# Stick-breaking attention: the values' products of two key blocks issued one behind the other

## The chip, the cores and the metric

The kernel runs on one core of a Trainium2 chip. Its time is the device time of one execution in microseconds (us); a kernel is timed several times and the median is given.

## What is computed

Three transformer blocks are applied to a sequence of 512 tokens of width 1024, all in float32. The first has stick-breaking attention with 16 heads of 64, the second has differential attention, the third mixes pooling, attention and a state-space scan; each ends in a gated feed-forward. The change touches only the attention of the first block:

```python
def block(args):
    q_blk, blk = args
    q_pos = blk * Q_BLOCK + jnp.arange(Q_BLOCK, dtype=jnp.int32)
    z = jnp.einsum('bqhd,bkhd->bhqk', q_blk, k, preferred_element_type=jnp.float32) * scale
    earlier = key_pos[None, :] < q_pos[:, None]
    log_keep = jnp.where(earlier, jax.nn.log_sigmoid(-z), 0.0)
    log_after = lax.cumsum(log_keep, axis=3, reverse=True) - log_keep
    weight = jnp.where(earlier, jnp.exp(jax.nn.log_sigmoid(z) + log_after), 0.0)
    return jnp.einsum('bhqk,bkhd->bqhd', weight.astype(v.dtype), v)
```

Every score z needs its softplus, and every weight needs the sum of the softplus values of all later keys. So the keys have to be gone through from the last to the first.

## The kernel before

TensorE (PE), VectorE (DVE), ScalarE (ACT) and the DMA queue (SP) each have a program of their own, written out by hand; semaphores tie them together. No scheduler moves anything: PE executes in the order in which the source names its steps.

Matrices with float32 accuracy are multiplied in three parts, since each operand is kept as a high and a low half: part 0 is high by high, part 1 the input's low half by the weights' high half, part 2 the input's high half by the weights' low half. `product` (line 1826) issues such a product of eight rows of 128 for one tile of 128 output columns: per part eight matmuls of 128x512 (L1844). `linear(n, j, parts)` is that product for head pair n, with j = 0, 1, 2 for query, key and value. The result is taken out of PSUM by DVE (`qkv_tile`, L1087), which also scales it.

The first block's attention runs over eight pairs of heads, n = 0 to 7. `pair(n, last)` in `stick_breaking` goes through the four key blocks of 128 of one pair, g = 0 to 3, from the last keys to the first. Key block g is seen by 128, 256, 384 or 512 queries. For each g:

- `scores(n, g)`: two matmuls of 64 contraction rows, one for each head of the pair, run side by side on the two halves of the array's rows (L1909), and then two small ones that add the mask (L1912). They write the PSUM pair `S2[g % 2]`.
- ACT's `soften(n, g)` (L589, L591, L593) takes the absolute value, the exponential and the logarithm of it. DVE's `softplus(n, g)` (L1101, L1103, L1105) finishes the softplus and splits it into `soft_hi` and `soft_lo`. For g = 0 to 2, DVE's `fold(n, g)` (L1113, L1116, L1119, L1121) adds up what the next key block needs, in the tile `later`.
- `exponents(n, g)`: PE adds the sums over later keys into the same PSUM pair: four matmuls from `soft_hi` and `soft_lo` (L1922), and for g > 0 two from `later` (L1927), with a wait of its own ahead of them.
- ACT's `weights(n, g)` (L598) takes the exponential and writes `wgt`. It signals `sb_w`.
- `weigh(n, g)`: two matmuls with 64 output columns, one for each head, run side by side on the two halves of the array's columns (L1940). They add up the output of the pair in the PSUM bank `ob`. They wait for `sb_w` (L1937), and for g = 0 also for `sb_o` (L1935, the bank `ob` has been read) and `sb_vt` (L1936, the values have been turned). Behind g = 3, DVE's `output(n)` reads `ob` (L1126, L1128).

`scores(n, g)` reuses a PSUM pair and so waits (L1906) until `weights` of two key blocks before has read it. `scores(n, 2)` therefore has the same condition on `sb_w` as `weigh(n, 0)`, `scores(n, 3)` as `weigh(n, 1)`, `scores(n + 1, 0)` as `weigh(n, 2)`, and `scores(n + 1, 1)` as `weigh(n, 3)`.

Between these steps of pair n, PE's program has parts of the query, key and value products of pair n + 1 (`fill`); in the last pair, parts of the output projection (`begin_out`, L1870) stand there. DVE's order in one pair is: softplus 1, fold 0, a weight split (L968), softplus 2, fold 1, the query tile, a split, the key tile (L1087), softplus 3, fold 2, a split, softplus 0 of pair n + 1, the value tile, `output(n)`, `values(n + 1)`. Each DVE instruction waits for the one before it where it reads its result.

Of the kernel before, what the change touches and what calls it, by code (L numbers as in the profile page):

```python
# [154 lines left out]
def three_blocks(nc, tables, x, positions, attn_norm, w_in, w_out, q_norm, k_norm, lambda_q1, lambda_k1,  # L155
# [19 lines left out]
    with ctx:  # L175
# [1647 lines left out]
        def _(pe):  # L1823
# [34 lines left out]
            def begin_out(l, f, parts, rows=range(KT - 1)):  # L1858

                u, acc = At(U_WO[l] + f), out_bank(l, f)  # L1860
                wh, wl = w_hi[u.slot], w_lo[u.slot]
                for part in parts:
                    if part == 0:
                        pe.wait_ge(hi_ready, u.of(1, 1))
                        if f < 2 and 0 in rows:
                            pe.wait_ge(evac, V_WO[l] + f + 1)
                    if part == 2:
                        pe.wait_ge(lo_ready, u.of(1, 1 + CREDIT))
                    for k in rows:
                        ins = pe.matmul(acc[:, :], (wh, wh, wl)[part][:, k, :], (o_hi, o_lo, o_hi)[part][:, k, :],  # L1870
                                        start=part == 0 and k == 0, stop=False, skip_group_check=True)
                if f < 2 and 2 in parts and KT - 2 in rows:
                    ins.then_inc(lin_done, 1)
# [27 lines left out]
            def stick_breaking(u0, v0, late):  # L1901
                def scores(n, g):

                    j = NB - 1 - g
                    pe.wait_ge(evac, n.of(3, v0 + 2 + CREDIT))
                    pe.wait_ge(sb_w, (n.scale(4) + g).of(1, 1))  # L1906
                    for a in range(2):
                        k = slice(64 * a, 64 * a + 64)
                        pe.matmul(S2[g % 2][:, a, 0:SPAN[j]], kb[n.slot][k, P * j:P * j + P], qb[n.slot][k, P * j:SEQ],  # L1909
                                  start=True, stop=True)  # L1910
                    for a in range(2):
                        ins = pe.matmul(S2[g % 2][:, a, 0:P], mask("ident"), mask("hide_sb"), start=False, stop=True,  # L1912
                                        skip_group_check=True)
                    ins.then_inc(sb_z, 1)

                def exponents(n, g):

                    j = NB - 1 - g
                    pe.wait_ge(sb_soft, n.of(SB_SOFT[NB], SB_SOFT[g + 1]))
                    for a in range(2):  # L1920
                        for part in (soft_hi, soft_lo):
                            ins = pe.matmul(S2[g % 2][:, a, 0:SPAN[j]], table_r("neg_from"), part[:, a, OFF[j]:OFF[j] + SPAN[j]],  # L1922
                                            start=False, stop=True, skip_group_check=True)
                    if g:
                        pe.wait_ge(sb_later, n.of(SB_LATER[NB - 1], SB_LATER[g]))
                        for a in range(2):
                            ins = pe.matmul(S2[g % 2][:, a, P:SPAN[j]], table_r("neg_all"),  # L1927
                                            later[:, a, LATER[g - 1]:LATER[g - 1] + SPAN[j + 1]],
                                            start=False, stop=True, skip_group_check=True)
                    ins.then_inc(sb_exp_in, 1)  # L1930

                def weigh(n, g):
                    j = NB - 1 - g
                    if g == 0:
                        pe.wait_ge(sb_o, n.of(2, 1))  # L1935
                        pe.wait_ge(sb_vt, n.of(1, 1))  # L1936
                    pe.wait_ge(sb_w, (n.scale(4) + g).of(1, 1 + CREDIT))  # L1937
                    for a in range(2):
                        cols = slice(64 * a, 64 * a + 64)
                        ins = pe.matmul(ob[cols, P * j:SEQ], vt[n.slot][:, j, cols], wgt[:, a, OFF[j]:OFF[j] + SPAN[j]],  # L1940
                                        start=g == 0, stop=g == NB - 1, skip_group_check=True)
                    if g == NB - 1:
                        ins.then_inc(sb_pv, 1)

                def turn_values(n):
                    pe.wait_ge(evac, n.of(3, v0 + 3 + CREDIT))
                    pe.wait_ge(sb_vt, n.of(1))
                    for b in range(NB):
                        ins = pe.transpose(misc[:, b * P:(b + 1) * P], vf[:, b * P:(b + 1) * P], table("ident"))
                    ins.then_inc(sb_vtr, 1)  # L1950

                def linear(n, j, parts=(0, 1, 2), late=None):
                    product(n.scale(3) + (u0 + j), n.scale(3) + (v0 + j), h_hi, h_lo, parts=parts, late=late)

                def pair(n, last):

                    def fill(j, parts):
                        if not last:
                            linear(n + 1, j, parts)
                        else:  # L1960
                            if j == 0 and 0 in parts:
                                pe.wait_ge(sb_o, n.of(2, 1))
                            if j == 2 and 0 in parts:
                                pe.wait_ge(sb_vt, n.of(1, 1))
                            begin_out(0, j, parts)
                    exponents(n, 0)
                    fill(0, (0,))
                    weigh(n, 0)
                    scores(n, 2)
                    fill(0, (1, 2))  # L1970
                    exponents(n, 1)
                    fill(1, (0,))
                    weigh(n, 1)
                    scores(n, 3)
                    fill(1, (1, 2))
                    exponents(n, 2)
                    fill(2, (0,))
                    weigh(n, 2)
                    if not last:
                        scores(n + 1, 0)  # L1980
                    fill(2, (1,))
                    exponents(n, 3)
                    fill(2, (2,))
                    weigh(n, 3)
                    if last:
                        begin_out(0, 3, (0,))
                    if not last:
                        scores(n + 1, 1)
                        turn_values(n + 1)
# [27 lines left out]
                turn_values(At(0))  # L2017
                pe.wait_ge(vec_ready, 2)
                by_two(pe, KT, pair)

            def differential(u0, v0, late):
# [457 lines left out]
```

## Time and profile before

| what | value |
|---|---|
| median of 3 runs | 2180.82 us (2180.41 to 2181.83) |
| the profiled execution's own time | 2181.55 us |
| its span on the core | 2179.8 us |
| granted TensorE clock, mean | 0.998 of full speed |
| PE busy | 2155.2 us (99%) |
| DVE busy | 1418.8 us (65%) |
| ACT busy | 792.1 us (36%) |
| DMA | 188.31 MB, mean 86 GB/s |

The span is what the profiler saw on the core from the first to the last instruction. Busy shares are of the span. Matmuls overlap in the records, since the next is issued before the one before has left the array; so the cost of a matmul in a row of matmuls is read from start to start. Where a timeline row says "x4" for two matmuls in the program, it is because a float32 matmul shows as two passes.

### The profile page before, as it was taken

How to read it: one execution, taken by the hardware profiler on the slowest of the kernel's cores; microseconds unless marked ns; L12 is line 12 of the kernel's file. 1: busy time of each engine (PE TensorE's matmuls, PEld its weight loads, DVE VectorE, ACT ScalarE, POOL GpSimd, SP SyncE). 2: the span in 40 equal slices, each digit the busy share in tenths (PEclk: the TensorE clock that was granted, in tenths of full speed). 3: DMA queues.
4: the chain of work that ended last, by engine and by line, in shares of the span. 5: the costliest groups of instructions: out<-in, count | busy, mean ns of one | idle time of the engine just before them, and what ended most of it. 6: DMA issues, size and time to landing. Idle time of an engine off the chain costs nothing.

```text
span 2179.8 us, 28415 instructions
## 1 busy us (share of the span) xinstructions
PE 2155.2 (99%) x10090; PEld 1720.2 (79%) x10090; DVE 1418.8 (65%) x2154; ACT 792.1 (36%) x1165; POOL 0.2 (0%) x4
## 2 busy tenths in 40 slices
PE   8999999999999999999999999999999999999998
PEld 6666788888887777888888877777788888888887
DVE  7888855554448897655554486687755567888733
ACT  6555422222225555322222234366622223222222
POOL 0000000000000000000000000000000000000000
PEclk9999999999999999999999999999999999999999
DMA  4212233333332222333333322222233333333332
GB/s 145 58 58 58 68 97 96 96 96 92 97 93 58 67 68 59 104 97 97 96 95 88 102 77 59 58 78 69 68 97 96 97 100 93 96 96 96 102 97 92
DMA packets 367252, 188.31 MB, mean 86 GB/s; under 512 B 8984, under 2 KB 366409, under 8 KB 367177
## 3 DMA queue, kind: packets, MB, share of 16 engines
q1 hardware_dynamic: 367177, 187.30, 30.1%
q8 instruction: 49, 0.80, 0.2%
q14 instruction: 26, 0.21, 0.0%
HBM read 185.18 MB, written 2.10 MB: 86 GB/s over the span
## 4 chain that ended last, share of the span: by engine, by line
PE 89%; DVE 7%; ACT 2%; issue 1%; DMA 0%; SPq 0%; DVEq 0%; ACTq 0%
PE lin L1844 79%; PE S L2029 1%; PE S L1909 1%; DVE conv L1486 1%; PE ob L2064 1%; PE lin L1870 1%; PE ob L1940 1%; ACT w_hi L553 1%; PE S L1870 1%; ACT L838 0%; PE misc L2042 0%; PE S L2205 0%; DVE soft_lo L1105 0%; DVE soft L1101 0%; PE ob L2230 0%
## 5 line engine op out<-in xcount | busy, mean ns | idle before, releaser
L553 ACT ACTIVATE w_hi<-raw 128x1024 fp32r<-128x1024 f32 x361 | 381.5, 1057 | 831.8 <-PE lin L1844 806.5
L968 DVE TENSOR_TENSOR w_lo<-raw,w_hi 128x1024 fp32r<-128x1024 f32 x361 | 441.1, 1222 | 208.2 <-ACT w_hi L553 206.7
L1844 PE MATMUL lin<-h_hi,w_hi 128*128 128x512 f32 x1928 | 490.8, 396 | 0.4
L1844 PE MATMUL lin<-h_lo,w_hi 128*128 128x512 f32 x1928 | 485.0, 393 | 0.0
L1844 PE MATMUL lin<-h_hi,w_lo 128*128 128x512 f32 x1928 | 477.9, 390 | 0.0
L1844 PEld LDWEIGHTS lin<-h_hi,w_hi 128*128 128x128 f32 x1928 | 359.3, 189 | 81.6 <-issue 8.0
L1844 PEld LDWEIGHTS lin<-h_hi,w_lo 128*128 128x128 f32 x1928 | 361.0, 188 | 74.4
L1844 PEld LDWEIGHTS lin<-h_lo,w_hi 128*128 128x128 f32 x1928 | 358.9, 188 | 76.7 <-issue 3.8
L1844 PE MATMUL lin<-gu_lo,w_hi 128*128 128x512 f32 x528 | 131.4, 389 | 0.0
L1844 PE MATMUL lin<-gu_hi,w_lo 128*128 128x512 f32 x528 | 131.4, 389 | 0.0
L1844 PE MATMUL lin<-gu_hi,w_hi 128*128 128x512 f32 x528 | 131.3, 389 | 0.0
L1310 DVE TENSOR_TENSOR up<-lin,rsB 128x512 f32<-128x512 f32 x44 | 30.4, 692 | 134.5 <-PE lin L1844 134.5
L1844 PEld LDWEIGHTS lin<-gu_hi,w_lo 128*128 128x128 f32 x528 | 99.1, 188 | 20.6
L1844 PEld LDWEIGHTS lin<-gu_lo,w_hi 128*128 128x128 f32 x528 | 99.1, 188 | 20.5
L1844 PEld LDWEIGHTS lin<-gu_hi,w_hi 128*128 128x128 f32 x528 | 99.1, 188 | 20.5
L1693 DVE SCALAR_TENSOR_TENSOR cout<-cpad,vec,cout 128x512 f32<-128x512 f32 x88 | 66.2, 752 | 12.0 <-DVE cout L1690 1.5
L1307 DVE TENSOR_TENSOR gate<-lin,rsB 128x512 f32<-128x512 f32 x44 | 30.4, 692 | 62.9 <-PE lin L1844 57.9
L558 ACT ACTIVATE sq<-xt 128x512 f32<-128x512 f32 x32 | 20.3, 633 | 130.8 <-DVE xt L986 94.5
L1657 DVE TENSOR_TENSOR g_raw<-lin,rsB 128x512 f32<-128x512 f32 x21 | 14.5, 692 | 51.3 <-PE lin L1844 51.3
L589 ACT ACTIVATE soft_t<-S 128x256 f32<-128x256 f32 (+3 forms) x32 | 22.6, 707 | 56.7 <-PE S L1912 56.6
L986 DVE TENSOR_TENSOR xt<-lin,xT 128x512 f32<-128x512 f32 x24 | 16.6, 692 | 39.9 <-PE lin L1844 39.9
L889 ACT ACTIVATE gate_s<-cout 128x512 f32<-128x512 f32 x22 | 14.0, 634 | 71.2 <-DVE cout L1693 71.2
(400 smaller groups left out, 2203.1 us busy)
## 6 DMA issues: line engine op xcount, KB each, us to landing
raw<-in_w_in_dram SPq DMA_DIRECT2D x108, 512.0 KB, 3.7
raw<-in_w_gate_dram SPq DMA_DIRECT2D x44, 512.0 KB, 3.8
raw<-in_w_up_dram SPq DMA_DIRECT2D x44, 512.0 KB, 3.8
raw<-in_ffn_up_dram SPq DMA_DIRECT2D x44, 512.0 KB, 3.8
raw<-in_w_down_dram SPq DMA_DIRECT2D x32, 512.0 KB, 3.8
raw<-in_w_out_dram SPq DMA_DIRECT2D x24, 512.0 KB, 3.7
raw<-in_ffn_down_dram SPq DMA_DIRECT2D x16, 512.0 KB, 3.7
raw<-in_w_down_dram SPq DMA_DIRECT2D x16, 384.0 KB, 3.4
```

Of the source, the lines that this page charges most:

```text
L553: act.activation(w_hi[u.slot][:, :, :], raw[u.slot][:, :, :], ACT.Copy).then_inc(hi_ready, 1)
L589: act.activation(soft_j, S2[g % 2][:, :, 0:SPAN[j]], ACT.Abs).then_inc(sb_soft_t, 1)
L968: dve.tensor_tensor(w_lo[u.slot][:, :, :], raw[u.slot][:, :, :], w_hi[u.slot][:, :, :].bitcast(f32), ALU.subtract).then_inc(lo_ready, 1)
L1307: dve.tensor_tensor(gate[:, :], lin[v.slot][:, :], rsB[:, :], ALU.mult).then_inc(evac, 1)
L1310: dve.tensor_tensor(up[:, :], lin[(v + 1).slot][:, :], rsB[:, :], ALU.mult).then_inc(evac, 1)
L1486: s.did(dve.scalar_tensor_tensor(conv[:, :], convB[:, k:k + SEQ], w[k], conv[:, :], ALU.mult, ALU.add))
L1693: s.did(dve.scalar_tensor_tensor(cout[j][:, :], cpad[j][:, k:k + SEQ], col[k], cout[j][:, :], ALU.mult, ALU.add))
L1844: ins = pe.matmul(acc, (wh, wh, wl)[part][:, k, :], (hi, lo, hi)[part][:, k0 + k, :], start=first and part == 0 and k == 0, stop=last and ...
L1870: ins = pe.matmul(acc[:, :], (wh, wh, wl)[part][:, k, :], (o_hi, o_lo, o_hi)[part][:, k, :], start=part == 0 and k == 0, stop=False, skip_ ...
L1909: pe.matmul(S2[g % 2][:, a, 0:SPAN[j]], kb[n.slot][k, P * j:P * j + P], qb[n.slot][k, P * j:SEQ], start=True, stop=True)
L1940: ins = pe.matmul(ob[cols, P * j:SEQ], vt[n.slot][:, j, cols], wgt[:, a, OFF[j]:OFF[j] + SPAN[j]], start=g == 0, stop=g == NB - 1, skip_gr ...
L2029: pe.matmul(dst[:, 0:N], qb[n.slot][rows_, P * i:P * i + P], kb[n.slot][rows_, 0:N], start=True, stop=True)
```

## The change

Only the order in which `pair` issues its steps on PE is changed. `weigh(n, 0)` is moved behind `exponents(n, 1)` and the first part of the next product, directly ahead of `weigh(n, 1)`. `weigh(n, 2)` is moved to the end of the pair, directly ahead of `weigh(n, 3)`. The numbers of instructions on every engine are the same, and the orders on DVE, ACT, GpSimd and the DMA queue are the same.

```diff
                     exponents(n, 0)
                     fill(0, (0,))
-                    weigh(n, 0)
                     scores(n, 2)
                     fill(0, (1, 2))
                     exponents(n, 1)
                     fill(1, (0,))
+                    weigh(n, 0)
                     weigh(n, 1)
                     scores(n, 3)
                     fill(1, (1, 2))
                     exponents(n, 2)
                     fill(2, (0,))
-                    weigh(n, 2)
                     if not last:
                         scores(n + 1, 0)
                     fill(2, (1,))
                     exponents(n, 3)
                     fill(2, (2,))
+                    weigh(n, 2)
                     weigh(n, 3)
```

PE in the first half of a pair in the loop, before. `ob<-wgt,vt` is `weigh`, `S<-qb,kb` with `S<-masks` is `scores`, `lin<-h_hi,w_hi` is part 0 of a product and `lin<-h_lo,w_hi` part 1; the rows without a matmul are the register instructions of a wait.

```order
L1844 MATMUL lin<-h_hi,w_hi_54 128x512 x8
L1935 REGISTER_ALU
L1936 REGISTER_ALU
L1937 REGISTER_ALU
L1940 MATMUL ob<-wgt,vt_94 64x128 x2
L1909 MATMUL S<-qb_89,kb_91 128x384 x2
L1912 MATMUL S<-masks 128x128 x2
L1844 MATMUL lin<-h_lo,w_hi_54 128x512 x8
```

And in the changed kernel, the same place and then the place to which the step went:

```order
L1844 MATMUL lin<-h_hi,w_hi_54 128x512 x8
L1906 REGISTER_ALU
L1909 MATMUL S<-qb_89,kb_91 128x384 x2
L1912 MATMUL S<-masks 128x128 x2
L1844 MATMUL lin<-h_lo,w_hi_54 128x512 x8
```

```order
L1844 MATMUL lin<-h_hi,w_hi_54 128x512 x8
L1935 ISA
L1936 ISA
L1940 MATMUL ob<-wgt,vt_93 64x128 x2
L1937 REGISTER_ALU
L1940 MATMUL ob<-wgt,vt_93 64x256 x2
L1909 MATMUL S<-qb_88,kb_90 128x512 x2
```

The 128-query product has left its place ahead of the scores of key block 2 and stands directly ahead of the 256-query product.

PE in the second half of a pair, from the product of 384 queries to the matmuls on `later`, before:

```order
L1940 MATMUL ob<-wgt,vt_93 64x384 x2
L1909 MATMUL S<-qb_89,kb_91 128x128 x2
L1912 MATMUL S<-masks 128x128 x2
L1844 MATMUL lin<-h_lo,w_hi_55 128x512 x8
L1919 REGISTER_ALU
L1922 MATMUL S<-soft_hi,exact 128x512
L1922 MATMUL S<-soft_lo,exact 128x512
L1922 MATMUL S<-soft_hi,exact 128x512
L1922 MATMUL S<-soft_lo,exact 128x512
L1925 REGISTER_ALU
L1927 MATMUL S<-later,exact 128x384 x2
```

And in the changed kernel, from the matmuls on `later` on:

```order
L1927 MATMUL S<-later,exact 128x384 x2
L1840 REGISTER_ALU
L1844 MATMUL lin<-h_hi,w_lo_57 128x512 x8
L1940 MATMUL ob<-wgt,vt_93 64x384 x2
L1937 REGISTER_ALU
L1940 MATMUL ob<-wgt,vt_93 64x512 x2
L1909 MATMUL S<-qb_89,kb_91 128x256 x2
```

The 384-query product stood ahead of the wait for `later` (L1925) and now stands behind it, after one more part of a product.

## Rows read from the trace of the kernel before

**Rows 1.** The page: the span, and the busy time of each engine.
```profile
span 2179.8 us, 28415 instructions
PE 2155.2 (99%) x10090; PEld 1720.2 (79%) x10090; DVE 1418.8 (65%) x2154; ACT 792.1 (36%) x1165; POOL 0.2 (0%) x4
```

**Rows 2.** Waits from 30 to 256 us: waiting and releasing line: total us, times, longest.
```profile
DVE kb L1087 <- PE lin L1844: 15.8, 7, 2.5
PEld S L1927 <- DVE later L1121: 4.8, 8, 0.9
```

**Rows 3.** PE, one pair: start us, duration us, engine, line, operation, tiles, shapes, count.
```profile
119.95 0.44 PE L1940 MATMUL ob<-wgt,vt 128*64 128x128 f32 x4
120.32 0.92 PE L1909 MATMUL S<-qb,kb 64*128 64x384 f32 x4
...
127.63 0.65 PE L1940 MATMUL ob<-wgt,vt 128*64 128x256 f32 x4
128.21 1.13 PE L1909 MATMUL S<-qb,kb 64*128 64x512 f32 x4
...
133.12 0.34 PE L1922 MATMUL S<-soft_hi,exact 128*128 128x384 f32 x1
...
136.00 0.87 PE L1940 MATMUL ob<-wgt,vt 128*64 128x384 f32 x4
136.79 0.49 PE L1909 MATMUL S<-qb,kb 64*128 64x128 f32 x4
...
139.70 0.40 PE L1922 MATMUL S<-soft_hi,exact 128*128 128x512 f32 x1
139.94 0.39 PE L1922 MATMUL S<-soft_lo,exact 128*128 128x512 f32 x1
140.46 0.62 PE L1927 MATMUL S<-later,exact 128*128 128x384 f32 x2
...
142.86 1.08 PE L1940 MATMUL ob<-wgt,vt 128*64 128x512 f32 x4
143.87 0.70 PE L1909 MATMUL S<-qb,kb 64*128 64x256 f32 x4
```

**Rows 4.** DVE in the same pair; in brackets its idle time and the releaser.
```profile
133.31 0.69 DVE L1087 SCALAR_TENSOR_TENSOR kb<-lin,rsB 128x512 f32<-128x512 f32 x1 [2.47 <-PE lin L1844]
133.92 1.22 DVE L1101 SCALAR_TENSOR_TENSOR soft<-S,soft_t 128x1024 f32<-128x1024 f32 x1
...
135.90 1.23 DVE L1105 TENSOR_TENSOR soft_lo<-soft,soft_hi 128x1024 fp32r<-128x1024 f32 x1
...
139.45 0.95 DVE L1121 TENSOR_TENSOR later<-soft_t,later 64x768 fp32r<-64x768 f32 x1
```

**Rows 5.** ACT in the same pair: the weights of key blocks 0 and 2.
```profile
119.16 0.36 ACT L598 ACTIVATE wgt<-S 128x256 f32<-128x256 f32 x1
...
134.25 0.81 ACT L598 ACTIVATE wgt<-S 128x768 f32<-128x768 f32 x1 [1.44 <-PE S L1927]
```

**Rows 6.** PE in the third block: products of 512, 384, 256, 128 columns back to back.
```profile
1326.23 2.37 PE L2230 MATMUL ob<-fprobT,fvt 128*64 128x512 f32 x16
1328.54 0.42 PE L2242 MATMUL misc<-tab,fd_z 16*128 16x16 f32 x4
```

**Rows 7.** The last pair, all engines, in order of time.
```profile
238.73 1.03 ACT L589 ACTIVATE soft_t<-S 128x1024 f32<-128x1024 f32 x1 [1.96 <-PE S L1912]
...
241.97 1.23 DVE L1101 SCALAR_TENSOR_TENSOR soft<-S,soft_t 128x1024 f32<-128x1024 f32 x1 [1.63 <-ACT soft_t L593]
...
247.66 0.39 PE L1922 MATMUL S<-soft_lo,exact 128*128 128x512 f32 x1
...
248.52 0.62 PE L1927 MATMUL S<-later,exact 128*128 128x384 f32 x2 [0.47 <-DVE later L1121]
...
251.82 0.69 DVE L1126 TENSOR_SCALAR o_hi<-ob 128x512 fp32r<-128x512 f32 x1 [2.10 <-PE ob L1940]
...
253.45 0.40 PE L1886 MATMUL lin<-o_hi,w_hi 128*128 128x512 f32 x1
```

## The prediction

> **What bounds the kernel now.** The page comes first: PE is busy 2155.2 of 2179.8 us [rows 1]. With so little idle time on PE, the time changes by what PE's own stream of work gains or loses, and by the places where PE has to stand still. Every such place in the attention of the first block has to be found, because the change only moves PE's steps around.
>
> The list of waits over the eight pairs gives one line in which PE waits for another engine again and again: the matmuls on `later` (L1927) wait for DVE's last instruction of a fold (L1121), 8 times, once per pair [rows 2]. Its 4.8 us are idle time of the weight-load records and overstate what PE loses. The timeline of PE gives the loss itself: the matmuls of 512 columns on `soft_hi` and `soft_lo` start 0.24 us apart (139.70, 139.94), and the one on `later` behind them starts 0.52 us later, at 140.46 [rows 3]. So PE stands still for 0.52 - 0.24 = 0.28 us in this pair; the timeline shows the same distance in seven pairs. In the last pair the same distance is 248.52 - 247.66 = 0.86 us, so the wait there is about 0.62 us [rows 7].
>
> Next I read who sets the moment at which `later` is there. DVE's L1121 ends at 139.45 + 0.95 = 140.40, and PE's matmul starts 0.06 us later [rows 3, 4]. Going back along DVE, the chain begins with the key tile at 133.31, for which DVE had been idle for 2.47 us, waiting for the end of PE's product of the next pair's key [rows 4]; this wait occurs 7 times [rows 2]. Behind it softplus 3 and fold 2 run back to back, though softplus 3 has nothing to do with the key tile: it only stands behind it in DVE's order. So from the end of the key product to the matmuls on `later` there is a fixed time: DVE's chain. On PE's clock it runs from the first row of exponents 2 (133.12, the next thing that PE does behind the key product) to 140.46, which is 7.34 us [rows 3]. PE's own work in this stretch is 7.34 - 0.28 = 7.06 us. **The stretch is bound by DVE, with PE's work only just shorter.** The stream outside it is bound by PE. The product of 384 columns stands inside the stretch.
>
> **The change, part by part.** A product's price is read from its start to the start of what follows it: 120.32 - 119.95 = 0.37 us for 128 columns, 0.58 for 256, 0.79 for 384 and 1.01 for 512 [rows 3]. Each 128 columns add 0.21 to 0.22 us, which leaves about 0.16 us per group that does not depend on its size.
>
> *What a join saves.* The trace of before has no two of these products behind each other in this attention, but it has the same form in the third block: 512, 384, 256 and 128 columns back to back, with 64 output columns each. They take 1328.54 - 1326.23 = 2.31 us [rows 6], against 1.01 + 0.79 + 0.58 + 0.37 = 2.75 us for the four standing alone. Three joins save 0.44 us, so one saves 0.15 us. The bounds are nothing (a join saves nothing) and 0.16 us (the whole part that does not depend on size). I take 0.15, since the row has the same shapes, tiles and types. The Trainium skill, page "TensorEngine Tiling (Array Packing)", section "Key Properties", says that changing the tiling mode of the array drains it. By that rule each join removes one change of mode, and 16 joins are all the change does: a gain. The size of that gain is in the rows above, and the sum does not need the rule.
>
> *The first join (128 with 256 columns).* `weigh(n, 0)` leaves the place ahead of `scores(n, 2)`. Those scores then wait for the same signal, the weights of block 0, and reach that wait at 119.95 instead of 120.32. ACT finished them at 119.16 + 0.36 = 119.52 [rows 3, 5], so 0.43 us is left and no wait appears. `scores(n, 2)` start 0.37 us earlier, which helps no one who is late: DVE was idle for 2.47 us ahead of the key tile. Seen from the start of the pair, everything from `scores(n, 3)` on comes 0.15 us earlier. This is PE's time outside DVE's stretch: **-0.15 us per pair.**
>
> *The second join (384 with 512 columns).* This has two parts. Inside DVE's stretch PE loses 0.79 us of work and does 7.06 - 0.79 = 6.27 us, but the stretch still takes 7.34 us, since nothing of DVE's chain starts earlier: its beginning hangs on the end of the key product, and the distance from `scores(n, 3)` to that end is unchanged. The wait at L1927 grows from 0.28 to 1.07 us. Removing the product here gains nothing; it had been filling that wait. Behind the stretch, the product comes back at 0.79 - 0.15 = 0.64 us, where PE is the bound. So this part costs **+0.64 us per pair**.
>
> What stands behind the longer wait on PE does not turn it into more: the scores of the next pair now start at 136.00 instead of 136.79 and need the weights of block 2 (done at 134.25 + 0.81 = 135.06) and the key tile (133.31 + 0.69 = 134.00) [rows 4, 5]; exponents 3 start about 0.79 us earlier, at about 138.4, and need `soft_lo` (135.90 + 1.23 = 137.13) [rows 4]. ACT's weights of block 3 follow the matmuls on `later` as before. `scores(n + 1, 1)`, the turned values and DVE's `output(n)` follow the products as before, 0.64 us later as seen from L1927, and so does all that hangs on them.
>
> *The last pair.* There is no key tile; DVE's chain starts at 241.97, released by ACT, whose work started at 238.73 behind the mask of `scores(n, 3)` [rows 7]. So the fixed time starts at `scores(n, 3)`, which come 0.15 us earlier by the first join, and the rest is the same: `weigh(n, 2)` leaves a stretch that waits anyway and comes back behind it for 0.64 us. The end of `ob` is read by DVE from 251.82 and the projection's last rows start at 253.45 [rows 7], both shifted by the same amount.
>
> *The sum.* Per pair -0.15 + 0.64 = +0.49 us, in all 8 pairs: **+3.9 us**. Nothing before or behind the attention changes, and PE is busy 99% of the span, so the shift is carried to the end. The profiled execution took 2181.55 us, 0.73 us more than the median; it becomes 2185.5, and the median 2180.82 becomes **2184.7 us**, +0.18%. A measurement of this kernel can tell about 0.2%, or 4.4 us, from no change; the forecast is a loss just inside that.
>
> **The rivals.**
>
> *A. Joins save nothing.* The products keep their 0.79 us wherever they stand, and the moved one is paid in full behind the wait: 8 x 0.79 = +6.3 us, 2187.1 us. For it speaks that register instructions of a wait stand between the two products here. Against it speak the rows of the third block [rows 6].
>
> *B. Only the joins count.* `later` arrives 0.79 us earlier as well, or the wait turns out to be set by something that the change moves forward: 16 x 0.15 = -2.4 us, 2178.4 us. This is the result that the Trainium skill's rule on changes of tiling mode would give if nothing else in the pair mattered. What would decide it is where DVE's chain begins: if softplus 3 were held by ACT and not by the key tile, an earlier `scores(n, 3)` would pull it forward. It could then gain at most the 0.15 us by which those scores move. The bracket of 2.47 us at the key tile speaks against it [rows 4]. A partial form, in which the wait grows by less than 0.79 us, gives something between -2.4 and +3.9.
>
> *C. A new wait at `scores(n, 2)`.* These scores would have to wait for ACT's weights of block 0. The margin is 0.43 us [rows 3, 5], and ACT's work there follows `scores(n, 1)`, whose distance to this place changes only by the missing product, already counted. From the point at which the margin is used up each 0.1 us more costs 0.8 us over the kernel; a loss of 0.2 us per pair would give 3.9 + 1.6 = +5.5, 2186.3 us.
>
> *D. The order has no effect.* The wait grows by what the product gives up and the product comes back for as little as 0.3 us, so that the two joins pay for it: 2180.8 us. I see no row for that.
>
> **How the numbers follow.** The forecast, with terms of the sum off by no more than 0.1 us per pair (0.8 us in all), has a chance of 0.8. A has 0.07, C 0.05, B 0.03 and D and partial forms 0.05. The forecast lies 0.5 us below the 0.2% mark of 2185.2, and a median of a few runs is itself uncertain by about 0.7 us (the three runs shown span 1.4 us). So the forecast's own 0.8 divides into 0.57 within the mark and 0.23 beyond it. With A and C, slower by over 0.2% gets 0.35. Faster by over 0.2% would take 4.4 us, more than all joins together, and gets 0.02; within 0.2% gets the other 0.63 (0.57, and B, D and the partial forms but for these 0.02). The range goes from 2183.0 (both joins 0.1 us better than taken, and the spread of the median) to 2187.1 (A).
>
> **What would show it.** In the profile of the changed kernel: the distance from the last matmul on `soft_lo` to the matmul on `later` is 1.3 us in seven pairs instead of 0.52, and DVE's time from the key tile to the end of L1121 is unchanged at 7.1 us, with idle time of about 2.5 us ahead of the key tile. Two joined products take 0.80 us (128 with 256 columns) and 1.65 us (384 with 512) from start to start of what follows. `scores(n, 2)` follow part 0 of the product with no gap. From one pair to the next it takes 0.5 us more. The prediction is wrong if the wait at L1927 grows by clearly less than 0.79 us, if the joined products take as long as before, or if a wait shows elsewhere in the pair.

## The result and the profile after

| | before | changed |
|---|---|---|
| median | 2180.66 us (19 runs, 2179.73 to 2182.08) | 2185.17 us (19 runs, 2183.75 to 2186.89) |
| span of the profiled execution | 2179.8 us | 2181.9 us |
| ratio to before | | 1.002, 95% interval 1.0014 to 1.0026 |

The change costs 4.5 us, which is 0.21%; by the interval it lies between 3.1 and 5.7 us. The forecast was a loss of 3.9 us, and a median of 2184.7.

The waits of the changed kernel from 30 to 256 us, with the same columns as [rows 2]:

```profile
DVE kb L1087 <- PE lin L1844: 16.9, 7, 2.7
...
PEld S L1927 <- DVE later L1121: 11.5, 8, 1.9
...
PE S L1927 <- DVE later L1121: 8.0, 8, 1.5
```

PE's own wait at L1927 was long enough for a row in this list only once before, in the last pair [rows 7]. Now it has 8 entries and 8.0 us.

PE in one pair of the changed kernel, which answers to [rows 3]:

```profile
121.04 0.92 PE L1909 MATMUL S<-qb,kb 64*128 64x384 f32 x4
...
128.34 0.87 PE L1940 MATMUL ob<-wgt,vt 128*64 128x128 f32 x8
129.14 1.13 PE L1909 MATMUL S<-qb,kb 64*128 64x512 f32 x4
...
134.03 0.34 PE L1922 MATMUL S<-soft_hi,exact 128*128 128x384 f32 x1
...
136.91 0.49 PE L1909 MATMUL S<-qb,kb 64*128 64x128 f32 x4
...
140.05 0.39 PE L1922 MATMUL S<-soft_lo,exact 128*128 128x512 f32 x1
141.37 0.62 PE L1927 MATMUL S<-later,exact 128*128 128x384 f32 x2 [0.93 <-DVE later L1121]
141.83 2.01 PE L1844 MATMUL lin<-h_hi,w_lo 128*128 128x512 f32 x8
143.77 1.72 PE L1940 MATMUL ob<-wgt,vt 128*64 128x384 f32 x8
145.42 0.70 PE L1909 MATMUL S<-qb,kb 64*128 64x256 f32 x4
```

The joined products take 129.14 - 128.34 = 0.80 us and 145.42 - 143.77 = 1.65 us. A joined row counts x8 and carries the shape of its first member. The stretch from exponents 2 to the matmuls on `later` is 141.37 - 134.03 = 7.34 us, as before, and the distance at its end has grown from 0.52 to 141.37 - 140.05 = 1.32 us. The bracket says 0.93 and not the growth of 0.80 nor the wait of 1.08, because it counts from the modelled end of the matmul before; start to start is the measure.

DVE in the same pair, as in [rows 4]:

```profile
134.23 0.69 DVE L1087 SCALAR_TENSOR_TENSOR kb<-lin,rsB 128x512 f32<-128x512 f32 x1 [2.68 <-PE lin L1844]
134.84 1.21 DVE L1101 SCALAR_TENSOR_TENSOR soft<-S,soft_t 128x1024 f32<-128x1024 f32 x1
...
140.36 0.95 DVE L1121 TENSOR_TENSOR later<-soft_t,later 64x768 fp32r<-64x768 f32 x1
```

The chain takes 140.36 + 0.95 - 134.23 = 7.08 us, against 7.09 before. It still starts with the key tile and is still idle ahead of it.

The matmuls on `later` of two neighbouring pairs start at 113.40 and 141.37: one pair takes 27.97 us.

```profile
113.40 0.62 PE L1927 MATMUL S<-later,exact 128*128 128x384 f32 x2 [0.93 <-DVE later L1121]
```

In the kernel before, the same matmuls lie 27.50 us apart in every pair of the loop, so a pair costs 0.47 to 0.48 us more. From the first exponents of the attention to the first matmul of the projection's last rows (L1886) the two profiled executions take 218.5 and 222.2 us: +3.7 us. All the stages from there to the state-space scan of the third block differ by less than 0.1 us each. The span grew by only 2.1 us, for reasons that lie outside this attention; they are in the last section.

### The profile page after: what moved, and what is told of

It is laid out like the page before. It is cut to its first block, busy times and chain, and to the rows that moved or that the text cites. A ratio compares the mean times of both kernels' runs of the same rounds, so it can differ in the third digit from the quotient of the medians.

```text
span 2181.9 us, 28409 instructions
## 1 busy us (share of the span) xinstructions
PE 2150.9 (99%) x10090; PEld 1720.9 (79%) x10090; DVE 1418.4 (65%) x2154; ACT 791.7 (36%) x1165; POOL 0.2 (0%) x4
## 4 chain that ended last, share of the span: by engine, by line
PE 89%; DVE 7%; ACT 2%; issue 1%; DMA 0%; SPq 0%; DVEq 0%; ACTq 0%
PE lin L1844 78%; PE S L2029 1%; PE S L1909 1%; PE ob L1940 1%; DVE conv L1486 1%; PE ob L2064 1%; PE lin L1870 1%; ACT w_hi L553 1%; PE S L1870 1%; ACT L838 0%; PE misc L2042 0%; PE S L2205 0%; DVE soft_lo L1105 0%; DVE soft L1101 0%; PE ob L2230 0%
## 5 line engine op out<-in xcount | busy, mean ns | idle before, releaser
L598 ACT ACTIVATE wgt<-S 128x256 f32<-128x256 f32 (+3 forms) x32 | 22.4, 701 | 50.9 <-PE S L1927 50.9
```

The source lines that it names most:

```text
L598: act.activation(wgt[:, :, OFF[j]:OFF[j] + SPAN[j]], S2[g % 2][:, :, 0:SPAN[j]], ACT.Exp).then_inc(sb_w, 1)
```

## The experiments

All expectations were written before the runs. Three accounts were to be told apart: the forecast (the stretch up to `later` is bound by DVE, and a join saves 0.15 us), rival A (joins save nothing) and rival B (only joins count).

**1. The first join alone.**

```diff
                     fill(0, (0,))
-                    weigh(n, 0)
                     scores(n, 2)
...
                     fill(1, (0,))
+                    weigh(n, 0)
                     weigh(n, 1)
```

> Only the product of key block 0 is moved, to stand directly ahead of that of key block 1; that of key block 2 keeps its place. Theory (DVE bounds the stretch from the key product's end to the matmuls on later, a join saves 0.15 us): -0.15 us in each of 8 pairs, -1.2 us against the kernel before; a pair takes 27.35 us instead of 27.50; the distance at L1927 stays at 0.52 us. Rival A (joins save nothing): 0. Rival B (only joins count): -1.2 us. So this run tells A from the others.

Measured: 2179.50 us against 2180.98, which is -1.5 us; ratio 0.9995, interval 0.9986 to 1.0004. The time alone doesn't tell -1.2 from 0. The trace does, since all pairs of the loop take the same time to 0.01 us. The matmuls on `later` of two pairs:

```profile
112.03 0.62 PE L1927 MATMUL S<-later,exact 128*128 128x384 f32 x2
...
126.30 0.87 PE L1940 MATMUL ob<-wgt,vt 128*64 128x128 f32 x8
127.10 1.13 PE L1909 MATMUL S<-qb,kb 64*128 64x512 f32 x4
...
138.81 0.39 PE L1922 MATMUL S<-soft_lo,exact 128*128 128x512 f32 x1
139.33 0.62 PE L1927 MATMUL S<-later,exact 128*128 128x384 f32 x2
```

The pair takes 139.33 - 112.03 = 27.30 us, 0.20 less than before. The joined products take 0.80 instead of 0.37 + 0.58 = 0.95 us, which is the 0.15 of the forecast. The other 0.05 us is in the parts of linear products: the eight matmuls of one part take 0.02 to 0.03 us less in two places (1.91 instead of 1.93 us behind `scores(n, 3)`, 1.91 instead of 1.94 ahead of the product of 512 columns). Why is not explained here. The distance at L1927 stays at 0.52 us, since nothing inside the stretch was moved. The trace puts rival A out.

**2. The second join alone.**

```diff
                     fill(2, (0,))
-                    weigh(n, 2)
                     if not last:
                         scores(n + 1, 0)
...
                     fill(2, (2,))
+                    weigh(n, 2)
                     weigh(n, 3)
```

> Only the product of key block 2 is moved, to the pair's end ahead of that of key block 3; that of key block 0 keeps its place. Theory: the distance at L1927 grows from 0.52 to 1.32 us and the joined products take 1.65 us, so +0.64 us in each of 8 pairs, +5.1 us. Rival A: +0.79 x 8 = +6.3 us. Rival B: -1.2 us.

Measured: 2186.64 against 2180.98 us, +5.7 us; ratio 1.0027, interval 1.0017 to 1.0036, which is 3.7 to 7.9 us. Rival B is out by the sign. In the trace:

```profile
114.28 0.62 PE L1927 MATMUL S<-later,exact 128*128 128x384 f32 x2 [0.94 <-DVE later L1121]
...
141.06 0.39 PE L1922 MATMUL S<-soft_lo,exact 128*128 128x512 f32 x1
142.39 0.61 PE L1927 MATMUL S<-later,exact 128*128 128x384 f32 x2 [0.94 <-DVE later L1121]
```

A pair takes 28.11 us, +0.61 against the forecast's +0.64, and the distance is 1.33 us against 1.32. So the two halves of the change go in opposite directions: -0.20 and +0.61 us per pair, with a sum of +0.41, against +0.48 for both together; the small savings in the linear parts don't add up exactly.

**3. Three products together inside the stretch.** If the wait is what the moved product had been covering, then the joins should be made there.

```diff
                     fill(0, (0,))
-                    weigh(n, 0)
                     scores(n, 2)
...
                     fill(1, (0,))
-                    weigh(n, 1)
                     scores(n, 3)
...
                     fill(2, (0,))
+                    weigh(n, 0)
+                    weigh(n, 1)
                     weigh(n, 2)
```

> The products of key blocks 0 and 1 are both moved to stand directly ahead of that of key block 2, so three are joined inside the stretch that DVE bounds, and none has to go behind it. Theory: PE's work inside the stretch grows from 7.06 to 7.71 us and is over DVE's 7.34, so the wait of 0.28 us is gone, and two joins save 0.30: -0.58 us in 7 pairs and -0.9 us in the last (its wait of 0.62 us is covered as well), -5.0 us in all; the distance at L1927 falls to 0.23 us, a pair takes 26.9 us. Rival A: only the waits go, -0.28 x 7 - 0.62 = -2.6 us. Rival B: two joins as in the change, -2.4 us.

Measured: 2175.73 against 2180.98 us, -5.3 us; ratio 0.9975, interval 0.9966 to 0.9984. It is faster than both kernels.

```profile
111.02 0.52 PE L1927 MATMUL S<-later,exact 128*128 128x384 f32 x2
...
133.00 1.52 PE L1940 MATMUL ob<-wgt,vt 128*64 128x128 f32 x12
134.44 0.49 PE L1909 MATMUL S<-qb,kb 64*128 64x128 f32 x4
...
137.59 0.40 PE L1922 MATMUL S<-soft_lo,exact 128*128 128x512 f32 x1
137.82 0.52 PE L1927 MATMUL S<-later,exact 128*128 128x384 f32 x2
138.18 2.01 PE L1844 MATMUL lin<-h_hi,w_lo 128*128 128x512 f32 x8
```

The three products take 1.44 us, two joins less than the 1.74 of the three alone. The distance at L1927 is 0.23 us, as between any two matmuls there: no wait. A pair takes 137.82 - 111.02 = 26.80 us, 0.70 less, where 0.58 was expected. Most of the rest is in one row: the two matmuls on `later` take 138.18 - 137.82 = 0.36 us to what follows, where they take 0.46 behind a wait (140.46 to 140.92 before, 141.37 to 141.83 in the changed kernel). So in the pairs of the loop a wait costs what one sees ahead of it and 0.10 us more behind it. Why is not shown, and it is not a fixed price: in the last pair, where another product follows, the same two matmuls take 0.46 us behind the wait of before (248.52 to 248.98) and 0.44 here with no wait (242.77 to 243.21).

**4. The changed kernel with DVE's chain started earlier.** The prediction says that the chain starts late only because softplus 3 stands behind the key tile in DVE's order. Here the key tile goes between softplus 3's first and second instruction; everything is computed as before.

```diff
-                def softplus(n, g):
+                def softplus(n, g, between=None):
...
                     s.did(dve.scalar_tensor_tensor(soft[:, :, blk], S2[g % 2][:, :, 0:N], 0.0, soft_t[:, :, blk], ALU.max, ALU.add))
+                    if between:
+                        between()
                     s.settle()
...
-                        qkv_tile(n + 1, 1)
-                    softplus(n, 3)
+                    softplus(n, 3, None if last else lambda: qkv_tile(n + 1, 1))
```

> The changed kernel with one step of DVE's order moved: the next pair's key tile stands behind the first instruction of softplus 3 (L1101) instead of ahead of it. Theory: L1101 then starts when ACT is done, about 0.5 us ahead of the key product's end, and the chain to later ends 0.45 us earlier; the distance at L1927 falls from 1.32 to about 0.87 us in 7 pairs, -3.2 us against the change, +1 to +1.3 us against the kernel before. If the chain were held by ACT or by anything but its place behind the key tile, nothing would change and the time would stay at +4.5 us.

Measured: 2180.53 against 2180.98 us, -0.5 us; ratio 0.9998, interval 0.9989 to 1.0007. Against the changed kernel's median that is -4.6 us, more than the 3.2 expected; in the traces, from the first exponents to L1886, it is -4.2 us. DVE and PE (lines are one or two higher here, L1928 is the matmul on `later`):

```profile
132.94 1.23 DVE L1101 SCALAR_TENSOR_TENSOR soft<-S,soft_t 128x1024 f32<-128x1024 f32 x1 [2.21 <-ACT soft_t L593]
134.08 0.68 DVE L1087 SCALAR_TENSOR_TENSOR kb<-lin,rsB 128x512 f32<-128x512 f32 x1
134.68 0.69 DVE L1105 TENSOR_SCALAR soft_hi<-soft 128x1024 fp32r<-128x1024 f32 x1
```

```profile
133.21 0.34 PE L1923 MATMUL S<-soft_hi,exact 128*128 128x384 f32 x1
...
139.23 0.39 PE L1923 MATMUL S<-soft_lo,exact 128*128 128x512 f32 x1
139.96 0.61 PE L1928 MATMUL S<-later,exact 128*128 128x384 f32 x2 [0.34 <-DVE later L1123]
```

The idle time ahead of the chain's first instruction is now released by ACT (at L1101) and no longer by PE (at L1087), and the fixed stretch is 139.96 - 133.21 = 6.75 us instead of 7.34. So the chain was held by its place in DVE's order, and that is what bounded PE. The chain gained 0.59 us and not 0.45: I had not taken off the 0.1 us by which a DVE instruction starts ahead of the recorded end of the one before it when it doesn't wait for its result (134.08 against 132.94 + 1.23 = 134.17). The distance at L1927 is 139.96 - 139.23 = 0.73 us.

**5. The kernel before with DVE's chain started earlier.** The same DVE edit, with PE's order of before.

> The kernel before with only DVE's order moved: the next pair's key tile behind the first instruction of softplus 3. Theory: the chain from the key product's end to later gets 0.59 us shorter (as it did in the changed kernel), 6.75 us against PE's 7.06 us of work in the stretch, so the wait of 0.28 us at L1927 is gone in 7 pairs, the distance there falls from 0.52 to 0.23 us, and the time by 7 x 0.28 = 2.0 us. If the shorter chain were worth its full 0.59 us wherever it stands, it would be -4.1 us.

Measured: 2178.12 against 2180.95 us, -2.8 us; ratio 0.9987, interval 0.9978 to 0.9996.

```profile
132.15 0.34 PE L1923 MATMUL S<-soft_hi,exact 128*128 128x384 f32 x1
...
138.97 0.40 PE L1923 MATMUL S<-soft_lo,exact 128*128 128x512 f32 x1
139.20 0.52 PE L1928 MATMUL S<-later,exact 128*128 128x384 f32 x2
139.56 2.01 PE L1845 MATMUL lin<-h_hi,w_lo 128*128 128x512 f32 x8
```

The distance is 0.23 us, so the wait is gone, and the matmuls on `later` take 0.36 us again. With the 0.10 us behind the wait the saving is 0.39 us per pair and 2.7 us in seven, which is what was measured; the expectation of 2.0 counted only the wait. The stretch now takes 139.20 - 132.15 = 7.05 us, where PE's work in it had been worked out as 7.06. It is not the full 4.1 us by which DVE's chain got shorter: below PE's own work the chain is worth nothing. The last pair has no key tile to move, and its distance stays at 0.84 us.

**6. Three products together and DVE's chain started earlier.**

> The kernel with three joined products inside the stretch, and the key tile behind the first instruction of softplus 3. Theory: that kernel has no wait left at L1927 (0.23 us from start to start), so a shorter DVE chain is worth nothing: 0 against that kernel, -5.2 us against the kernel before, a pair 26.8 us. If DVE's chain still held PE in some way that the distance doesn't show, up to 0.59 x 7 = 4.1 us more would be gained.

Measured: 2175.86 against 2180.95 us, -5.1 us; ratio 0.9978, interval 0.9969 to 0.9987. That is 0.1 us from experiment 3. In a kernel with no wait at L1927, the same DVE edit that was worth 2.8 us in the kernel before and 4.6 us in the changed one is worth nothing that can be measured. The three results together put a number on the cover: with three joined products PE has 7.06 - 0.79 + 1.44 = 7.71 us of work in the stretch, and DVE's chain can be 7.34 or 6.75 us long without being seen.

The traces give the eight kernels a second time, by the time from the first exponents of the attention to L1886 in one profiled execution each. The medians have an interval of about 2 us in either direction or less; the traces show differences of the attention alone.

| kernel | attention in the trace, us | against before | median against before |
|---|---|---|---|
| before | 218.5 | | |
| the change | 222.2 | +3.7 | +4.5 |
| 1, first join | 216.9 | -1.5 | -1.5 |
| 2, second join | 223.4 | +4.9 | +5.7 |
| 3, three inside the stretch | 212.6 | -5.9 | -5.3 |
| 4, change, chain earlier | 218.0 | -0.5 | -0.5 |
| 5, before, chain earlier | 215.7 | -2.8 | -2.8 |
| 6, three, chain earlier | 212.6 | -5.9 | -5.1 |

## Why the prediction was right

*What bounds the kernel.* Right. The stretch from the end of the key product to `later` took 7.34 us before and 7.34 us in the changed kernel, though PE had 0.79 us less to do in it. Experiments 4 and 5 moved the bound by moving the key tile on DVE and touching nothing else: 6.75 us with the change's order on PE, and 7.05 us, PE's own work, with the order of before.

*The first join, -0.15 us per pair.* The joined products took 0.80 instead of 0.95 us, as read from the third block's row. The pair gained 0.20 us in experiment 1; the difference is in the linear parts and was not foreseen. `scores(n, 2)` start 1.98 us behind the start of the part ahead of them, as the product did before: no wait, so rival C did not come.

*The second join, +0.64 us per pair.* Experiment 2 gave +0.61. The wait grew by 0.80 us, and the joined products took 1.65 us.

*The last pair.* The time came out as forecast and one part of the account did not. Behind the matmuls on `later` the way to L1886 got 0.60 us longer (4.93 to 5.53), where 0.64 had been forecast. The wait ahead of them, however, grew by 1.01 us and not by 0.79: to 1.48 us by the bracket, against 0.47 [rows 7]. PE had lost more work than the product's 0.80 us from start to start. Here the product stands between two parts of the output projection with no scores behind it; before:

```profile
244.44 0.87 PE L1940 MATMUL ob<-wgt,vt 128*64 128x384 f32 x4
245.24 1.89 PE L1870 MATMUL misc<-o_lo,w_hi 128*128 128x512 f32 x7
246.97 0.39 PE L1922 MATMUL S<-soft_hi,exact 128*128 128x512 f32 x1
```

And without it, in the changed kernel:

```profile
245.54 1.78 PE L1870 MATMUL misc<-o_hi,w_hi 128*128 128x512 f32 x7
247.16 1.77 PE L1870 MATMUL misc<-o_lo,w_hi 128*128 128x512 f32 x7
248.77 0.39 PE L1922 MATMUL S<-soft_hi,exact 128*128 128x512 f32 x1
```

The part behind it takes 1.61 instead of 1.73 us and the one ahead of it 1.62 instead of 1.71 (before, it starts at 242.73). So the price read from start to start leaves out 0.2 us that the product costs its neighbours here. It made no difference to the time, because DVE's chain covers this stretch:

```profile
251.33 0.61 PE L1927 MATMUL S<-later,exact 128*128 128x384 f32 x2 [1.48 <-DVE later L1121]
```

*The sum.* +0.49 us per pair was forecast, the trace shows +0.48 in the loop, and the attention as a whole is 3.7 us longer. The medians say 4.5 us with an interval from 3.1 to 5.7, so 3.9 is inside it; the 0.8 us between the medians and the traces is within that interval, and nothing here explains it further. Whether the loss is a little more or a little less than 0.2% is not settled by these runs.

*The rivals.* A is refuted by the 0.15 us in experiments 1 to 3, although register instructions of a wait stand between the joined products; B by experiment 2. C did not come, and D, no effect of the order, is out by the interval, which starts at 3.1 us. The Trainium skill's rule that a change of tiling mode drains the array ("TensorEngine Tiling (Array Packing)", section "Key Properties") agrees in direction with these rows, 0.15 us for each change that a join removes; that the 0.15 us are such a drain and nothing else is not shown. The time of this kernel was decided by the wait and not by it: experiment 3 makes as many joins as the change and comes out 9.4 us faster.

Where the expectations of experiments 3 and 5 were off, it was mostly one term: in the loop a wait also slows the two matmuls directly behind it by 0.10 us. The prediction didn't suffer from it, since the wait at L1927 was there before and after, and that cost was paid in both.

## What to carry to other kernels

A step that fills a wait is not worth its own duration where it stands. Before moving it, find the releaser's chain, measure it from a fixed point of the waiting engine's stream, and compare it with the work that is left; here PE was already 0.28 us short of work in the stretch, and that told the sign. If there is something to gain by putting like steps together, put them together inside the wait: two joins there gave -5.3 us, of which about 2.4 by the joins and the rest by the wait that they covered, and two joins, one of which took its product out of the stretch, gave +4.5 us. And look at what the releasing engine does ahead of the chain, since one unrelated instruction there cost this kernel 2.8 us.

## What was not expected of the hardware

The spans of the two profiled executions differ by 2.1 us and the medians by 4.5. In part that is the choice of executions: the profiled one of the kernel before took 0.9 us more than its median, and that of the changed kernel, 2183.75 us, was the shortest of its 19. In the two traces the attention is 3.7 us longer, but 0.3 us are gained ahead of it, 0.2 us in the stages up to the scan, and 1.1 us in the state-space stage of the third block, which no edit touches. There PE waits about 2 us for DVE and then has a linear product. In the kernel before, PE in that place:

```profile
1550.53 0.66 PE L2334 MATMUL ob<-L,xd 128*64 128x128 f32 x8 [2.10 <-DVE L L1556]
...
1552.48 3.40 PE L1844 MATMUL lin<-h_hi,w_hi 128*128 128x512 f32 x8
```

And in the changed kernel:

```profile
1553.72 0.66 PE L2334 MATMUL ob<-L,xd 128*64 128x128 f32 x8 [2.10 <-DVE L L1556]
...
1555.40 2.11 PE L1844 MATMUL lin<-h_hi,w_hi 128*128 128x512 f32 x8
```

The same eight matmuls after the same idle time take 3.40 us in one and 2.11 us in the other. Busy time by stretch, with the granted clock behind the engines' columns, for the kernel before:

```profile
1550.00:1554.00 4.00, 3.47 (x32) 2.89 (x33) 3.50 (x6) 3.47 (x4) 0.00 (x0) 0.73 0.14 19
1554.00:1558.00 4.00, 4.00 (x15) 2.88 (x14) 3.90 (x7) 3.12 (x4) 0.00 (x0) 0.84 0.58 168
```

And for the changed kernel:

```profile
1554.00:1558.00 4.00, 3.80 (x37) 2.95 (x33) 3.73 (x6) 3.64 (x5) 0.00 (x0) 1.00 0.33 78
```

The granted clock was 0.73 and 0.84 there in the kernel before, a mean of full speed (2.4 GHz) and its half (1.2 GHz; from 1551.9 to 1555.2 us alone the profile gives 0.50), and 1.00 in the changed one. From the start of the scan's last L2312 to the end of DVE's last instruction, the profiled executions of the kernel before and of experiments 3, 5 and 6 take 636.8 us, all four with such a stretch of half clock, and those of the changed kernel and of experiments 1, 2 and 4 take 635.6 or 635.7 us, without one there. The two groups have no edit in common, and all eight have the wait of 2.0 to 2.1 us there. The 32 timed executions of the kernel before that stand beside experiments 1 to 4 have a mean granted clock between 0.997 and 1.000, so it differs also from one execution of the same program to the next. A span taken from one execution of this kernel therefore cannot be compared with another to better than 1 us. The attention has a granted clock of 1.00 throughout, also with the longer wait of the change.
